# In projection of a hybrid decoder: the convolution branch's tiles ahead of the recurrent ones, two recurrent gates a slot, norms and sums in other slots, the recurrence without its long reciprocal

## What is computed

```python
h = rmsnorm(x, norm1) * (1 + sc1) + sh1
proj = h @ w_in
a_val, a_gate, qkv, z, b_raw, a_raw, lru_x, lru_g = split(proj)      # 256, 256, 1536, 512, 4, 4, 256, 256

u = a_val * sigmoid(a_gate)                                          # convolution branch
u = causal_dwconv(u, s_conv_a, conv_a_w)                             # 31 taps
y_a = silu(layernorm(u + conv_a_b, ln_a_g, ln_a_b))

q, k, v = silu(causal_dwconv(qkv, s_qkv, conv_qkv_w))                # 4 taps; q and k are l2-normed
o, new_delta = gated_delta_chunked(q, k, v, g, beta, s_delta)        # delta branch

xc = causal_dwconv(lru_x, s_conv_lru, conv_lru_w) + conv_lru_b       # recurrent branch, 4 taps
r, i = sigmoid(xc @ w_a + b_a), sigmoid(xc @ w_i + b_i)
log_a = -8 * r * softplus(-lam);  a = exp(log_a)
b = sqrt(-expm1(2 * log_a)) * (i * xc);  h_t = a_t * h_(t-1) + b_t
y_c = rmsnorm(h * gelu(lru_g), lru_norm)
```

## Time and profile before

| what | value |
|---|---|
| median of 3 runs | 2149.41 us (2148.02 to 2151.97) |
| profiled execution | 2149.24 us, its span 2147.2 us |
| PE busy | 1899.6 us (88%) |
| DVE, ACT, POOL busy | 957.6, 703.4, 269.1 us |
| mean granted clock | 0.923 of full speed |
| in projection, layer 0 | 54.4 us to about 280 us |
| in projection, layer 1 | about 978 us to 1199 us |

### The profile page before, as it was taken

How to read it: one execution, slowest core, us unless ns; L and a number is a source line. 1 busy time by engine, 2 the same in 40 slices (tenths; PEclk the granted TensorE clock), 3 DMA queues, 4 the chain that set the end, 5 groups by cost and what they waited for, 6 DMA issues and landing times.

```text
span 2147.2 us, 40561 instructions
## 1 busy us (share of the span) xinstructions
PE 1899.6 (88%) x16248; PEld 1653.0 (77%) x16248; DVE 957.6 (45%) x1777; ACT 703.4 (33%) x1438; POOL 269.1 (13%) x450
## 2 busy tenths in 40 slices
PE   3999797897999999997996968984799999999983
PEld 3777566775999999996774657863689989989772
DVE  3269631524333233324596414322553735718434
ACT  3221342413222132222213423311543634617432
POOL 1028320300000000010085202001000000000001
PEclk9999897798999999998998977896899999999995
DMA  8455320022555355523342200203668869779663
GB/s 308 158 177 178 112 83 13 3 84 98 165 168 175 112 172 163 184 105 114 138 138 74 83 22 3 74 10 117 221 199 276 283 215 332 240 236 322 193 242 132
DMA packets 88028, 328.70 MB, mean 153 GB/s; under 512 B 10595, under 2 KB 11203, under 8 KB 86563
## 3 DMA queue, kind: packets, MB, share of 16 engines
q1 hardware_dynamic: 79778, 295.18, 41.1%
q0 software_dynamic: 5120, 20.43, 2.6%
q10 hardware_dynamic: 2944, 10.49, 1.4%
HBM read 276.59 MB, written 49.46 MB: 152 GB/s over the span
## 4 chain that ended last, share of the span: by engine, by line
PE 78%; POOL 7%; DVE 6%; issue 4%; ACT 2%; DMA 2%; SPq 0%; POOLq 0%; ACTq 0%; DVEq 0%
PE PB L815 10%; PE PB L817 9%; PE PB L816 9%; PE PB L1002 8%; PE PB L1003 7%; PE PB L953 7%; PE PB L950 7%; POOL TMP L2243 4%; PE PB L951 3%; POOL XA L2244 3%; PE PB L690 1%; PE PB L991 1%; PE PB L442 1%; PE PB L706 1%; PE PB L992 1%
## 5 line engine op out<-in xcount | busy, mean ns | idle before, releaser
L1002 PE MATMUL PB<-hT,ring 128*128 128x288 f32 x864 | 289.0, 417 | 18.9 <-ACT hT L1534 18.3
L1003 PE MATMUL PB<-hT,ring 128*128 128x288 f32 x864 | 284.1, 411 | 0.0
L815 PE MATMUL PB<-HH,VH 128*128 128x288 f32 x704 | 209.7, 298 | 17.6 <-DVE HL L1891 15.9
L1002 PEld LDWEIGHTS PB<-hT,ring 128*128 128x128 f32 x864 | 164.9, 194 | 67.0 <-ACT hT L1534 18.8
L950 PE MATMUL PB<-XX,UH 128*128 128x512 f32 (+3 forms) x704 | 213.0, 370 | 1.5 <-DVEq L1983 1.5
L816 PE MATMUL PB<-HL,VH 128*128 128x288 f32 x704 | 208.8, 297 | 0.0
L817 PE MATMUL PB<-HH,VL 128*128 128x288 f32 x704 | 208.0, 295 | 0.0
L1003 PEld LDWEIGHTS PB<-hT,ring 128*128 128x128 f32 x864 | 167.3, 194 | 47.2
L951 PE MATMUL PB<-XX,UL 128*128 128x256 f32 (+3 forms) x704 | 181.6, 258 | 0.0
L815 PEld LDWEIGHTS PB<-HH,VH 128*128 128x128 f32 x704 | 133.0, 189 | 18.2 <-issue 18.2
L950 PEld LDWEIGHTS PB<-XX,UH 128*128 128x128 f32 x704 | 132.1, 188 | 12.8 <-DVEq L1983 1.7
(11 more groups left out here) (482 smaller groups left out, 3646.9 us busy)
## 6 DMA issues: line engine op xcount, KB each, us to landing
SS<-in_w_ada SPq DMA_DIRECT2D x88, 512.0 KB, 5.8
ring<-in_moe_gu SPq DMA_DIRECT2D x88, 512.0 KB, 4.6
RX<-in_moe_gu SPq DMA_DIRECT2D x88, 512.0 KB, 4.6
ring<-in_w_in SPq DMA_DIRECT2D x48, 512.0 KB, 3.5
ring<-in_ffn_gu SPq DMA_DIRECT2D x46, 512.0 KB, 4.3
RX<-in_moe_dn SPq DMA_DIRECT2D x44, 512.0 KB, 4.6
ring<-in_moe_dn SPq DMA_DIRECT2D x44, 512.0 KB, 4.6
moe_in<-CO SPq DMA_DIRECT2D x30, 512.0 KB, 5.5
```

Source lines behind the costliest of these rows:

```text
L815: pe.matmul(out, a[0], b[0], start=first, stop=False)
L1002: mm(main[:, 0:HN], w, rows(k)[:, 0:HN], start=(k == 0), stop=(k == KD - 1))
L1003: end = mm(rest[:, 0:HN], w, rows(k)[:, HN:T], start=(k == 0), stop=(k == KD - 1))
```

## The change

The table of the tile order goes: tile p is in slot p, so the convolution branch has slots 0 to 3 and the recurrent one slots 4 to 7. On PE the cumulated gates move from slot 6 to 4, the four recurrent gates from slots 2 to 5 into slots 7 and 8 (two each, on the same banks), the recurrent norm's sums from 10 to 12, the layer norm's sums and the l2 sums one slot forward. ACT's parts follow. ACT also computes the decay a itself, as an exponential, which takes the place of DVE's reciprocal: with t the tanh of half its exponent, 1 / (1 + t) is (1 + a) / 2, so a = 1 - (a + 1) t, and b has the factor (a + 1) / 2. DVE's list has the gated product and `conv_a(0)` ahead of the recurrent convolutions, and the last `conv_q` behind the modulation. POOL no longer copies two tiles' state before its convolution.

```diff
-TILES = tuple(range(LRU_X, QKV)) + tuple(range(LRU_X)) + tuple(range(QKV, M_IN))
-PLACE = {m: p for p, m in enumerate(TILES)}
...
-            if 2 <= p < 6:
-                c, a = (p - 2) // 2, p % 2
-                if p == 2:
-                    pe.wait_ge(S["ab_gates"], l + 1)
-                    pe.wait_ge(S["in_small"], 16 * 8 * (l + 1))
-                else:
-                    pe.wait_ge(S["lru_t"], 6 * l + p - 2)
...
-            if p == 6:
-                pe.wait_ge(S["lru_t"], 6 * l + 4)
+            if p == 4:
+                pe.wait_ge(S["ab_gates"], l + 1)
                 pe.wait_ge(S["small_ready"], 4 * l + 2)
...
-            if p == 10:
-                pe.wait_ge(S["small_ready"], 4 * l + 3)
+            if p in (7, 8):
+                c = p - 7
+                for a in range(2):
+                    if 2 * c + a == 0:
+                        pe.wait_ge(S["small_ready"], 4 * l + 3)
+                        pe.wait_ge(S["in_small"], 16 * 8 * (l + 1))
+                    else:
+                        pe.wait_ge(S["lru_t"], 8 * l + 2 * c + a)
+                    pe.wait_ge(S["conv_l"], 4 * l + 2 * (c + 1))
+                    mm(PB[5][:, 0:HN], WL[:, a, c, :], XL[:, c, 0:HN], start=True, stop=True)
+                    mm(PB[6][:, 0:HN], WL[:, a, c, :], XL[:, c, HN:T], start=True, stop=True).then_inc(S["lru_g_pe"], 1)
+            if p == 12:
+                pe.wait_ge(S["lru_t"], 8 * l + 4)
                 for c in range(2):
                     pe.wait_ge(S["yc_sq"], 2 * l + c + 1)
...
-            if p in (15, 16):
+            if p in (14, 15):
                 for c in range(2):
-                    if p == 15:
+                    if p == 14:
...
-            if p == 17:
+            if p == 16:
                 pe.wait_ge(S["ln_mean"], 2 * (l + 1))
                 squares_summed(0)
-            if p == 18:
+            if p == 17:
                 sums_turned(0)
                 squares_summed(1)
-            if p == 19:
+            if p == 18:
                 sums_turned(1)
...
-            if 2 <= p < 6:
-                c, a = (p - 2) // 2, p % 2
-                act.wait_ge(S["lru_g_pe"], 4 * l + p - 1)
...
-            if p == 5:
-                act.wait_ge(S["lru_t"], 6 * l + 4)
+            if p in (7, 8):
+                c = p - 7
+                for a in range(2):
+                    act.wait_ge(S["lru_g_pe"], 4 * l + 2 * c + a + 1)
+                    bias, dst = LM[:, l, 6 + a, c:c + 1], (lru_r, lru_i)[a]
+                    fn(dst[:, c, 0:HN], PB[5][:, 0:HN], ACT.Tanh, scale=0.5, bias=bias)
+                    fn(dst[:, c, HN:T], PB[6][:, 0:HN], ACT.Tanh, scale=0.5, bias=bias).then_inc(S["lru_t"], 1)
+            if p == 8:
+                act.wait_ge(S["lru_t"], 8 * l + 4)
                 for c in range(2):
                     fn(lru_u[:, c, :], lru_r[:, c, :], ACT.Tanh, scale=LM[:, l, 5, c:c + 1], bias=LM[:, l, 5, c:c + 1]).then_inc(S["lru_t"], 1)
-                act.wait_ge(S["lru_t"], 6 * (l + 1))
+                act.wait_ge(S["lru_t"], 8 * l + 6)
+                for c in range(2):
+                    fn(lru_r[:, c, :], lru_r[:, c, :], ACT.Exp, scale=LM[:, l, 0, c:c + 1], bias=LM[:, l, 0, c:c + 1]).then_inc(S["lru_t"], 1)
                 fn(lru_b, lru_u, ACT.Sqrt).then_inc(S["lru_sqrt"], 1)
-            if p == 9:
-                for c in range(2):
...
-            if p == 10:
+            if p == 11:
+                for c in range(2):
...
-            if p == 15:
+            if p == 13:
                 for i in range(3):
                     silu_of(i)
+            if p == 14:
+                silu_of(3)
+                silu_of(4)
...
-                silu_of(9)
-            if p == 19:
+            if p == 18:
...
+                silu_of(9)
                 silu_of(10)
+            if p == 19:
                 silu_of(11)
...
-                    tile_out(TILES[p], PM[p % 2], PS[p % 2], p % 2)
+                    tile_out(p, PM[p % 2], PS[p % 2], p % 2)
...
-            conv_l(0)
             dve.wait_ge(S["ab_pe"], 2 * (l + 1))
...
-            conv_l(1)
             dve.wait_ge(S["small_exp"], 3 * (l + 1))
...
+            for c in range(2):
+                dve.wait_ge(free_s[c], t0 // 2 + 2)
+                sv = lambda ap: ap.rearrange("p (b c) -> p b c", c=WQ - 1 + NS)[:, :, WQ - 1:]
+                dve.scalar_tensor_tensor(UA[:, c, WA - 1:AO], pj[:, A_GATE + c, WQ - 1:SO], 1.0, pj[:, A_VAL + c, WQ - 1:SO], ALU.add, ALU.mult).then_inc(S["glu_ready"], 1)
...
+            dve.wait_ge(S["glu_ready"], 4 * (l + 1))
+            conv_a(0)
+            dve.wait_ge(S["gc_pe"], l + 1)
+            then(dve.tensor_copy(SM[:, 4, 0:16], gates_out[:, 0:16]))
...
+            dve.tensor_tensor(sm(7), sm(5), sm(4), ALU.subtract).then_inc(S["small_ready"], 1)
+
+            conv_l(0)
+            conv_l(1)
+            conv_a(1)
+            dve.wait_ge(S["lru_t"], 8 * (l + 1))
             dve.wait_ge(S["lru_sqrt"], l + 1)
-            tr, ti, tz, sq, hs = lru_r, lru_i, lru_u, lru_b, XL
-            then(dve.tensor_scalar(tr, tz, 1.0, None, ALU.add))
-            then(dve.reciprocal(tr, tr))
+            ae, ti, tz, sq, hs = lru_r, lru_i, lru_u, lru_b, XL
+            then(dve.scalar_tensor_tensor(tz, ae, 1.0, tz, ALU.add, ALU.mult))
+            then(dve.scalar_tensor_tensor(sq, ae, 1.0, sq, ALU.add, ALU.mult))
             then(dve.tensor_scalar(tz, tz, -1.0, 1.0, ALU.mult, ALU.add))
-            then(dve.tensor_tensor(tz, tz, tr, ALU.mult))
-            then(dve.tensor_tensor(sq, sq, tr, ALU.mult))
             then(dve.scalar_tensor_tensor(ti, ti, 1.0, XL[:], ALU.add, ALU.mult))
-            then(dve.tensor_tensor(sq, sq, ti, ALU.mult))
+            then(dve.scalar_tensor_tensor(sq, sq, 0.5, ti, ALU.mult, ALU.mult))
...
-            dve.wait_ge(S["gc_pe"], l + 1)
-            then(dve.tensor_copy(SM[:, 4, 0:16], gates_out[:, 0:16]))
...
-            dve.wait_ge(S["glu_ready"], 4 * (l + 1))
-            conv_a(0)
+            for i in range(3):
+                conv_q(i)
             dve.wait_ge(S["yc_sqrt"], 2 * (l + 1))
...
-            conv_a(1)
-            for i in range(4):
+            for i in range(3, 6):
                 conv_q(i)
...
-            for i in range(4, 8):
+            for i in range(6, 8):
                 conv_q(i)
...
-            for i in range(8, 12):
+            for i in range(8, 11):
                 conv_q(i)
-            dve.wait_ge(S["conv_q"], 24 * (l + 1))
-
             dve.wait_ge(S["small_exp2"], 6 * (l + 1))
...
             modulation(IN_BATCH[l])
+            conv_q(11)
+            dve.wait_ge(S["conv_q"], 24 * (l + 1))
...
+            then(dve.tensor_scalar(LM[:, :, 0, :], LM[:, :, 5, :], -2.0, None, ALU.mult))
...
-                for i in range(2):
-                    next_in(i)
-                    next_out(i)
...
-                for i in range(2, 14):
+                for i in range(14):
```

More of the change, by code:

```diff
@@ L470, in beside @@
                 mm(PB[6][0:TS, 32:40], RS[0:Q, P:P + TS], ident[0:Q, 0:8], start=True, stop=True).then_inc(S["ab_pe"], 1)
-            if 2 <= p < 6:
-                c, a = (p - 2) // 2, p % 2
-                if p == 2:
-                    pe.wait_ge(S["ab_gates"], l + 1)
-                    pe.wait_ge(S["in_small"], 16 * 8 * (l + 1))
-                else:
-                    pe.wait_ge(S["lru_t"], 6 * l + p - 2)
-                pe.wait_ge(S["conv_l"], 4 * l + 2 * (c + 1))
-                mm(PB[5][:, 0:HN], WL[:, a, c, :], XL[:, c, 0:HN], start=True, stop=True)
-                mm(PB[6][:, 0:HN], WL[:, a, c, :], XL[:, c, HN:T], start=True, stop=True).then_inc(S["lru_g_pe"], 1)
-            if p == 6:
-                pe.wait_ge(S["lru_t"], 6 * l + 4)
+            if p == 4:
+                pe.wait_ge(S["ab_gates"], l + 1)
                 pe.wait_ge(S["small_ready"], 4 * l + 2)
@@ L1129, in beside_act @@
                 fn(ELS[:], ELS[:], ACT.Exp).then_inc(S["small_exp2"], 1)
-            if p == 10:
+            if p == 11:
+                for c in range(2):
+                    act.wait_ge(S["lru_scan"], 2 * l + c + 1)
+                    fn(SQ[:, c, :], XL[:, c, :], ACT.Square).then_inc(S["yc_sq"], 1)
+            if p == 12:
                 act.wait_ge(S["yc_pe"], l + 1)
@@ L1157, in beside_act @@
                     fn(SQ[:, c, :], XA[:, c, :], ACT.Square).then_inc(S["ln_sq"], 1)
-            if p == 16:
+            if p == 15:
                 act.wait_ge(S["ln_sum"], 2 * l + 2)
@@ L1605, in conv_l @@
             def conv_l(c):
-                dve.wait_ge(free_s[c], t0 // 2 + 1)
+                dve.wait_ge(free_s[c], t0 // 2 + 3)
                 o = PC["conv_lru_w"][0] + c * WQ
```

38 lines of the change are left out of this document (13 added, 25 removed).

## The result

The changed kernel took 2117.49 us in the median of 4 runs (2115.70 to 2119.77) beside 2150.69 us of the kernel before (4 runs, 2148.02 to 2154.41). The ratio is 0.9845 with a 95% interval from 0.9826 to 0.9864: 33 us less. The forecast was 2116, from a sum of -33.6. The profiled execution of the changed kernel is the longest of the four (2119.77, its span 2117.9), so what is read from its trace sums to some 2 us less gain than the medians show.

What follows compares the result with a forecast made beforehand. PE's own queue was taken to bound the in projection, except where it stops for POOL. Terms -35.0 - 5.3 + 4.9 + 2.4 - 0.6 = -33.6 gave 2116 us for the median, range 2110 to 2127.

Steps and rivals of the forecast that it cites:

- Part 1: Convolution branch first: POOL starts its sample convolution earlier, PE's stops at the column sums vanish, -35.0 us, and -5.3 of clock.
- -5.3 for the clock: After PE's two stops, half of 5.35 and 5.25 us at half clock speed is lost; this goes: -5.3 us.
- the 101 us for the chain: POOL's sample convolution at the slow end, recurrence included, takes 101 us and is done at 197 in layer 0.
- The slow rate of 1.57 us a tap: POOL's tap beside DVE's taps, against 0.95 us with DVE idle; taken because DVE is busy nearly all through.
- Rival B: POOL stays last in layer 1; PE waits 6 us in slot 14 and the clock falls again: 2125 us, 9%.
- Part 2: Two recurrent gates in slots 7 and 8 share banks; PE pauses 1.2 us for ACT four times: +4.9 us.
- Part 3: Recurrence without DVE's reciprocal: DVE wins some 9 us a layer, worth nothing as PE does not wait: cost 0, at most 1.
- Part 4: Norms and sums one or two slots earlier: +2.4 us for the last turned sums, -0.6 for the modulation.
- +2.4 for the sums without cover: The last turned sums (1.24 us) no longer run while PE waits for POOL's diagonal: +2.4 us for two layers.
- The wait for the diagonal: Sign of being right: PE's wait for POOL's diagonal at the in projection's end grows from 4.6 to about 6.
- The -0.6 for the modulation: DVE's modulation ahead of the last q convolution: first z tile no longer waits 0.45 us, -0.6 for both layers.
- Part 5: Transfers of modulation weights between adjacent groups (slots 5 and 6, 10 and 11, layer 0): cost 0, at most 1 us each.

Runs made afterwards that it cites:

- experiment 2: The kernel before, in its old order, with POOL doing only 12 of 31 taps of each sample convolution (outputs differ): 2105.62 us, ratio 0.9801.
- experiment 5: The changed kernel with POOL doing only 12 of 31 taps of each sample convolution (outputs differ): 2115.39 us, ratio 0.9835.
- experiment 6: The changed kernel with the second recurrent gate of each pair issued in the middle of the next tile: 2114.47 us, ratio 0.9827.
- experiment 8: The changed kernel with the old recurrence: reciprocal and two more long operations on DVE, no exponentials on ACT: 2116.53 us, ratio 0.9849.
- experiment 7: The changed kernel with the last turned sums back in slot 19 and DVE's last q convolution ahead of the modulation: 2114.05 us, ratio 0.9834.
- experiment 3: The kernel before, tile table kept, with DVE forming the convolution branch's gated product ahead of the recurrence: 2145.17 us, ratio 0.9979.
- experiment 9: The changed kernel with layer 0's modulation groups moved so that the adjacent pairs 5, 6 and 10, 11 go: 2117.39 us, ratio 0.9840.
- experiment 10: The changed kernel with POOL writing the first chunk's two diagonals before it waits for the last tile's state: 2104.81 us, ratio 0.9791.
- experiment 11: The changed kernel with second gates half a tile later, modulation groups apart and POOL's first two diagonals earlier: 2095.88 us, ratio 0.9756.

## Why the prediction was right, by its own steps

**Part 1** carried the forecast and held. The stops of 35.0 us went, and -5.3 for the clock with them; experiment 2 gives 18.0 and 22.4 for stop and clock against 17.9 and 22.3. POOL started at 98.15 instead of "near 96", and was done at 187.86 instead of 197: the step that was off is the 101 us for the chain, which took 89.7. The sums, in turn, were reached at 208.48 and not at 205. The reason for POOL's part is in the rows of POOL by line, at 98 to 122 beside DVE's first 31-tap convolution and at 170 to 188 beside its short ones:

```profile
L2249 POOL TENSOR_SCALAR TMP<-UA,PA 128x64 f32<-128x64 f32 x15 | 12.4, 826 | 1.5
L2250 POOL TENSOR_TENSOR XA<-XA,TMP 128x64 f32<-128x64 f32 x15 | 8.5, 567 | 1.2
...
L2249 POOL TENSOR_SCALAR TMP<-UA,PA 128x64 f32<-128x64 f32 x13 | 8.7, 672 | 1.3
L2250 POOL TENSOR_TENSOR XA<-XA,TMP 128x64 f32<-128x64 f32 x14 | 6.9, 494 | 1.2
```

The slow rate of 1.57 us a tap holds where DVE runs 512-column taps without a break, and is too slow where short operations and waits lie between. I had taken it for all 62 taps to be safe, and the margins came out as 20.6 and 12.5 us instead of 8 and 4. Rival B, at 9% the largest, was further off than I said.

The Trainium skill (SBUF — State Buffer, Who interferes with whom) has the two engines exclude each other, and says that the order of issue decides who blocks. The runs agree for POOL, whose product takes 826 ns beside DVE's long taps and 445 with DVE idle. For DVE they agree in part: its long taps one behind the other take 752 ns with POOL at work and without, while those between short operations take 831 ns in the median beside POOL and 752 without it (experiment 5).

**Part 2** was put at +4.9, and experiment 6 gives 5.0 for it. PE stands idle four times for 0.98 us, 3.9 in all, but what was forecast, and what counts, is how much later its work goes on. In slot 8 of layer 0 the rows of the changed kernel are these:

```profile
150.88 0.50 ACT L1113 ACTIVATE QC<-PB,LM 128x288 f32<-128x288 f32 x1 [0.86 <-PE PB L488]
151.28 0.49 ACT L1114 ACTIVATE QC<-PB,LM 128x288 f32<-128x288 f32 x1
...
151.83 0.75 PE L487 MATMUL PB<-XL,WL 128*128 128x288 f32 x2 [0.98 <-ACT QC L1114]
```

ACT's two reads take 0.89 us (150.88 to 151.77), and PE is back 0.06 us later. I had allowed 0.15 for that signal and 0.2 for the one ahead of the reads. From the start of the first pair to the start of the second I had 2.32 us (106.58 to 108.9) and it is 2.20 to 2.22.

**Part 3** is 0, as said: experiment 8. That ACT's chain would delay DVE's start was not in the text, and did not matter.

**Part 4**: +2.4 for the sums without cover. Experiment 7, which puts them back, gives 2.2. By the rows, the distance from the last tile to the first matmul of the delta branch was 1.24 + 4.57 = 5.8 us before and is 5.4 to 5.8 now, behind a tile that starts 1.24 us later. The wait for the diagonal did grow from 4.6 to 5.4 and 5.8 ("about 6"). The -0.6 for the modulation holds: no wait stands ahead of the first z tile.

**Part 5** is the term that was mis-sized. I took 0 for the modulation weights in slots 6 and 11, with an upper bound of 1 us at each place. It is 0.7 to 2.4 us for the two, and single waits reached 1.62, beyond the bound. I had worked with one measured landing of 7.7 us against a gap of 8.1; the landings scatter by more than the 0.4 between them. (The four issues alone, which took SP 2.67 us in the row that I used, took 3.58 in the changed kernel's profile.) A margin so thin should have been priced at its mean shortfall, not at zero.

**The sum.** With what the experiments measured inside the stages: -40.6 (experiment 2) + 5.0 (experiment 6) + 2.2 (experiment 7) + 1.15 (the loads in this profile) = -32.3, against -32.2 read from the two profiles without their first tiles. The forecast for the stages was -33.0, that is -33.6 without the modulation, which lies behind them. It is 0.8 us off, and part 5 is the term that it lacked. The medians' -33.2 can't tell such differences: their interval reaches from 29 to 37 us, and that they lie within 0.4 of the forecast is luck. In the profiled execution alone 29.3 us are gained; 1.5 of what is missing are the first tile of layer 0.

## What to carry to other kernels

When an engine stands still for a slow helper, look for the earliest moment at which the helper's input can exist, and reorder the producer's tiles for that; reordering only the engine between (experiment 3) gave 5 us of 33. Cutting the helper's work in the old kernel (experiment 2) is a cheap test of the whole idea, and its distance to the changed kernel (here 4.5 and 3.9 us in the two stages) is the list of small costs that the new order brought: go through it, since here experiments 6 and 9 give more than half of it back. Then look at the next stop in line: a helper that does bookkeeping ahead of what the main engine waits for (experiment 10) was worth 13 us for a move of a few lines.

## What the runs showed of the hardware that I had not expected

**A stop's price in clock does not follow its length.** Stops of 0.98 us left the granted clock at 1.00, and so did the waits for modulation weights of up to 1.62 us; stops of 5.08, 14.84, 15.26 and 19.70 us were each followed by 4 to 6 us at 0.50 or 0.51, that is at 1.2 GHz. The 5.08 us stop was followed by the longest of these stretches (5.8 us). So shortening a long stop to 5 us leaves its clock cost standing; bringing it down to 1 us, as in experiment 10, takes that away. Between 1.62 and 4.57 us no stop was measured.

**The clock far behind the stage differed between profiles.** In two profiles the granted clock some 100 to 160 us after the in projection, in a stretch full of short waits, was higher. The windows of the changed kernel and of experiment 10, each 60 us, from 100 us after the first matmul of the delta branch (equal in time; the second holds a little more of the dense work that follows, as its DMA share shows):

```profile
368.01:428.01 60.00, 52.85 (x1141) 48.27 (x1140) 30.19 (x95) 24.31 (x91) 13.66 (x10) 0.69 0.01 3
```

```profile
363.15:423.15 60.00, 52.10 (x1165) 46.59 (x1164) 29.19 (x98) 28.13 (x108) 12.29 (x10) 0.83 0.09 36
```

Experiment 2 also had 0.83 there, experiment 11 had 0.74, the repetition of the changed kernel 0.72. From the in projection of layer 0 to that of layer 1 it took 688.57 us in experiment 10, 691.25 in experiment 2 and 692.64 in experiment 11, against 695 to 699 in all other profiles, that of the kernel before (697.19) included. Of this, 2.0 us in experiments 10 and 11 are only the half speed behind L554 that they are rid of, which lies in this stretch; that leaves experiment 11 with next to nothing, and experiments 2 and 10 with some 4 us or more. The medians of experiments 2 and 11 came out 3.5 and 4.0 us under what was expected; that of experiment 10 needs nothing of it, since its 12.9 us are accounted for in the two stages and the clock right behind them. Whether the kernels cause this or single executions fall so is open: each has one profile.

**A table load on ACT cost its 1.28 us and nothing beside.** In ACT's rows of experiment 8 the second load starts 0.02 us after the operation before it ends, and behind the first the next operation starts within 0.01 us.
